# A decoder layer's feed-forward blocks of seven products: one of the three weight sums is made by an accumulating DMA, the other three partial sums are split in one instruction

## What is computed

```python
def swiglu(x, w_gate, w_up, w_down):
    return (jax.nn.silu(x @ w_gate) * (x @ w_up)) @ w_down
...
h = layer_norm(ALPHA * h + 0.5 * swiglu(h, ffn1_w_gate, ffn1_w_up, ffn1_w_down), ln1_g, ln1_b)
mix = hybrid_mixer(h, ...)          # SSD branch, sliding-window attention, gated merge, output projection
h = layer_norm(ALPHA * h + mix, ln2_g, ln2_b)
h = layer_norm(ALPHA * h + 0.5 * swiglu(h, ffn2_w_gate, ffn2_w_up, ffn2_w_down), ln3_g, ln3_b)
```

## Time and profile before

| | us |
|---|---|
| median of 3 runs | 2670.63 |
| lowest, highest | 2668.64, 2671.52 |
| the profiled execution | 2668.99 |
| its span, first to last instruction | 2667.4 |
| PE busy in it | 2634.5 (99%) |
| DVE busy | 2002.6 (75%) |
| ACT busy | 1361.7 (51%) |
| mean granted TensorE clock | 0.996 |

### The profile page before, as it was taken

One profiled execution on the slowest core, in us unless ns is written; L12 is line 12 of the kernel. 1 busy time (PEld: TensorE's weight loads), 2 busy tenths in 40 slices (PEclk: granted clock), 3 DMA queues, 4 the chain that ended last, 5 costly groups with the idle time before them and its releaser, 6 DMA issues.

```text
span 2667.4 us, 36687 instructions
## 1 busy us (share of the span) xinstructions
PE 2634.5 (99%) x12546; PEld 2188.8 (82%) x12546; DVE 2002.6 (75%) x2410; ACT 1361.7 (51%) x1678; POOL 130.0 (5%) x170
## 2 busy tenths in 40 slices
PE   8999999999999999999999999999999999999997
PEld 7888888888787788888888888888878888888886
DVE  6999997688666665677777765444689999977986
ACT  5555555455344454566555554444355555554553
POOL 1000000000000000211111100000000000000000
PEclk9999999999999999999999999999999999999999
DMA  6666566666655546665555565667666665666664
GB/s 224 204 191 209 185 205 204 214 200 204 189 171 147 156 150 197 206 181 179 177 177 177 179 183 165 190 190 247 200 190 204 190 211 186 205 202 229 210 208 171
DMA packets 286195, 513.96 MB, mean 193 GB/s; under 512 B 19648, under 2 KB 52592, under 8 KB 284048
## 3 DMA queue, kind: packets, MB, share of 16 engines
q1 hardware_dynamic: 279552, 485.03, 57.8%
q0 software_dynamic: 4880, 25.36, 2.6%
q10 hardware_dynamic: 1664, 2.26, 0.2%
HBM read 506.23 MB, written 6.36 MB: 192 GB/s over the span
## 4 chain that ended last, share of the span: by engine, by line
PE 95%; DVE 3%; ACT 1%; issue 0%; DMA 0%; POOL 0%; POOLq 0%; SPq 0%; ACTq 0%; DVEq 0%
PE acc L787 13%; PE acc L789 13%; PE acc L788 13%; PE acc L853 5%; PE acc L855 5%; PE acc L854 5%; PE acc L871 4%; PE acc L872 4%; PE acc L873 4%; PE spare L871 4%; PE spare L872 4%; PE spare L873 4%; PE spare L855 3%; PE spare L854 3%; PE spare L853 3%; PE spare L756 2%
## 5 line engine op out<-in xcount | busy, mean ns | idle before, releaser
L1728 DVE TENSOR_TENSOR w_lo<-land,w_hi 128x1024 fp32r<-128x1024 f32 (+1 forms) x956 | 1149.2, 1219 | 499.4 <-ACT w_hi L1309 490.6
L1309 ACT ACTIVATE w_hi<-land 128x1024 fp32r<-128x1024 f32 (+1 forms) x956 | 976.8, 1029 | 916.9 <-PE acc L789 328.0
L787 PE MATMUL acc<-w_hi,a_hi 128*128 128x512 f32 (+1 forms) x1184 | 451.2, 381 | 2.6 <-DVE a_lo L1775 1.8
L789 PE MATMUL acc<-w_hi,a_lo 128*128 128x512 f32 (+1 forms) x1184 | 435.8, 368 | 0.0
L788 PE MATMUL acc<-w_lo,a_hi 128*128 128x512 f32 (+1 forms) x1184 | 434.4, 367 | 0.0
L787 PEld LDWEIGHTS acc<-w_hi,a_hi 128*128 128x128 f32 x1184 | 223.9, 189 | 46.8 <-issue 9.2
L789 PEld LDWEIGHTS acc<-w_hi,a_lo 128*128 128x128 f32 x1184 | 223.6, 189 | 38.2
L788 PEld LDWEIGHTS acc<-w_lo,a_hi 128*128 128x128 f32 x1184 | 224.1, 189 | 37.4 <-issue 3.6
L853 PE MATMUL acc<-w_hi,a_hi 128*128 128x512 f32 x576 | 227.7, 395 | 2.0 <-DVE a_lo L1775 1.7
L855 PE MATMUL acc<-w_hi,a_lo 128*128 128x512 f32 x576 | 225.1, 391 | 0.0
L854 PE MATMUL acc<-w_lo,a_hi 128*128 128x512 f32 x576 | 225.0, 391 | 0.0
(11 more groups left out here) (388 smaller groups left out, 4233.1 us busy)
## 6 DMA issues: line engine op xcount, KB each, us to landing
land<-w_in SPq DMA_DIRECT2D x232, 512.0 KB, 3.9
land<-ffn_w_gate SPq DMA_DIRECT2D x176, 512.0 KB, 3.9
land<-ffn_w_up SPq DMA_DIRECT2D x176, 512.0 KB, 4.3
land<-ffn_w_down SPq DMA_DIRECT2D x176, 512.0 KB, 4.7
land<-w_ssd_o SPq DMA_DIRECT2D x64, 512.0 KB, 4.3
land<-w_in SPq DMA_DIRECT2D x132, 128.0 KB, 2.3
land<-w_attn_o SPq DMA_DIRECT2D x32, 512.0 KB, 4.1
land<-w_out SPq DMA_DIRECT2D x32, 512.0 KB, 4.4
```

What stands on the lines that cost most here:

```text
L787: pe.matmul(to, rows_hi, hi, start=first, stop=False)
L789: mm = pe.matmul(to, rows_lo, hi, start=False, stop=last)
L1309: act.activation(w_hi[:, l % SPLIT, 0:deep, 0:width], land[:, l % LAND, 0:deep, 0:width], ACT.Copy).then_inc(high, 1)
L1728: dve.tensor_tensor(w_lo[:, l % SPLIT, 0:deep, 0:width], land[:, l % LAND, 0:deep, 0:width], w_hi[:, l % SPLIT, 0:deep, 0:width].bitcast(F ...
```

## The change

U0+U1 is no longer a DVE addition. After the first sum (now G0+U0, written to `t_sums` and not in place) POOL issues a DMA that reads U1 from HBM a second time, 256 KB, and adds it onto U0 in the landing buffer (`add_third`). The ordinary split of the up slab then splits (U0+U1, U1). ACT waits for that DMA (`third_added`) before it splits the up slab. The three sums that stay on DVE are contiguous in `t_sums`, and their high parts are made by one ACT instruction of 128x1536 and the low parts by one of DVE. Both stand ahead of the up slab's split in their engine's order, and PE takes the three products of the partial sums ahead of the two of the up slab.

```diff
+            def add_third(slot, n, block):
+                pool.wait_ge(sums, n * 3 + 1)
+                pool.dma_start(land[:, slot, 0, :], block, accum_op=ALU.add).then_inc(third_added, 16)
...
+            up_thirds(1)
             refill_late(1, x_view)
             hidden_complete(1)
             pool.dma_start(resid[:, :, 0:2 * W], x_view[:, :, 0:2 * W]).then_inc(resid_in, 16)
+            down_thirds(1)
...
                 pe.wait_ge(rest, slab_at + 1)
                 three(aux[:, 0, :], rows_of(0, 0), block(lg, 0), first, last)
                 three(own[:, 0, :], rows_of(1, 0), block(lg, 1)).then_inc(used, 1)
+                pe.wait_ge(t_rest, n + 1)
+                three(aux[:, 1, :], mixed_rows(1), t_block(0), first, last)
+                if turned is not None:
+                    pe.wait_ge(gt_out, turned)
+                three(aux[:, 3, :], mixed_rows(2), t_block(1), first, last)
+                three(own[:, 1, :], rows_of(1, 1), t_block(2)).then_inc(t_used, 1)
                 pe.wait_ge(rest, slab_at + 2)
                 three(own[:, 2, :], mixed_rows(3), block(lu, 1))
-                three(aux[:, 1, :], mixed_rows(1), block(lu, 0), first, last).then_inc(used, 1)
...
+                three(aux[:, 2, :], mixed_rows(0), block(lu, 0), first, last).then_inc(used, 1)
...
-                        act.wait_ge(sums, n * 4 + 2)
-                        split(f"up{f}", i, l)
+                    if n is not None and l % 2 == 1:
+                        act.wait_ge(third_added, n * 16 + 16)
+                    split(f"up{f}", i, l)
+                    if n is not None and l % 2 == 0:
                         t_high_parts(n, "up")
...
-                dve.tensor_tensor(sz[:, 0, :], up[:, 0, :], up[:, 1, :], ALU.add).then_inc(sums, 1)
-                dve.wait_ge(sums, n * 4 + 1)
-                dve.tensor_tensor(up[:, 0, :], gate[:, 0, :], up[:, 0, :], ALU.add).then_inc(sums, 1)
-                dve.wait_ge(sums, n * 4 + 2)
-                dve.tensor_tensor(sz[:, 1, :], up[:, 0, :], up[:, 1, :], ALU.add).then_inc(sums, 1)
-                dve.wait_ge(sums, n * 4 + 3)
+                dve.tensor_tensor(sz[:, 0, :], gate[:, 0, :], up[:, 0, :], ALU.add).then_inc(sums, 1)
+                dve.wait_ge(sums, n * 3 + 1)
+                dve.tensor_tensor(sz[:, 1, :], sz[:, 0, :], up[:, 1, :], ALU.add).then_inc(sums, 1)
+                dve.wait_ge(sums, n * 3 + 2)
                 dve.tensor_tensor(t_four, sz[:, 1, :], gate[:, 1, :], ALU.add).then_inc(sums, 1)
...
-                    split(f"up{f}", i, l)
                     if l // 2 in SEVEN and l % 2 == 1:
                         t_low_parts(seven_block(f, i, l // 2), "up")
+                    split(f"up{f}", i, l)
```

More of the change, by code:

```diff
@@ L349, in build_decoder_layer @@
         state = placed("state", [P, W], F32, 94 * K)
-        sz = sb("sz", [P, TOK, W])
-        bcT = sb("bcT", [P, 2, SEQ])
+        t_sums = sb("t_sums", [P, 3, W])
+        sz = t_sums[:, 0:TOK, :]
+        t_four = t_sums[:, TOK, :]
+        bcT = t_four.rearrange("p (k n) -> p k n", k=2)
         b_tok = sb("b_tok", [P, P])
@@ L651, in refill_late, with up_thirds, chunk, down_thirds @@
                 pool.dma_start(resid[:, :, 2 * W:], view[:, :, 2 * W:]).then_inc(resid_late_in, 16)
+            def add_third(slot, n, block):
+                pool.wait_ge(sums, n * 3 + 1)
+                pool.dma_start(land[:, slot, 0, :], block, accum_op=ALU.add).then_inc(third_added, 16)
+            def up_thirds(f):
+                def chunk(i):
+                    for b in SEVEN:
+                        add_third((2 * b + 1) % LAND, seven_block(f, i, b), ffn_w[f][1][:, 2 * b + 1, bass.ds(i * W, W)])
+                for i in range(1, ALONE + 1):
+                    chunk(i)
+                with pool.Fori(1, 1 + (NC_S - ALONE) // 2) as m:
+                    for k in range(2):
+                        chunk(m * 2 + (ALONE - 1 + k))
+            def down_thirds(f):
+                for j in range(2):
+                    for l, (p, c) in enumerate(DOWN_SLABS[j]):
+                        s = DOWN_ORDER[j][p]
+                        if s in DOWN_SEVEN and c == 1:
+                            at = (2 * j + 1) * W
+                            add_third(l % LAND, down_block(f, j, DOWN_SEVEN.index(s)),
+                                      ffn_w[f][2][:, 2 * s + 1, at:at + W])
+            up_thirds(1)
             refill_late(1, x_view)
@@ L1414, in t_high_parts @@
             def t_high_parts(n, t_set):
-                hi, hi_four, _, _ = t_of[t_set]
-                act.wait_ge(sums, n * 4 + 3)
+                act.wait_ge(sums, n * 3 + 3)
                 if not is_zero(n):
                     act.wait_ge(t_used, n)
-                act.activation(hi[:, :, :], sz[:, :, :], ACT.Copy).then_inc(t_high, 1)
-                act.wait_ge(sums, n * 4 + 4)
-                act.activation(hi_four[:, :], t_four, ACT.Copy).then_inc(t_high, 1)
+                act.activation(t_of[t_set][0][:, :, :], t_sums[:, :, :], ACT.Copy).then_inc(t_high, 1)
             def copy_one(f, i, odd):
-                act.wait_ge(t_used, seven_block(f, i, SEVEN[-1]) + 1)
+                act.wait_ge(used, slab_no(f"up{f}", i, 2 * SEVEN[-1] + 1) + 1)
                 act.activation(q_one, chunk_banks(1 - odd)[:, 0, :], ACT.Copy).then_inc(q_copied, 1)
@@ L1457, in copy_one_down @@
             def copy_one_down(f, j):
-                act.wait_ge(t_used, down_block(f, j, len(DOWN_SEVEN) - 1) + 1)
+                last = 2 * DOWN_ORDER[j].index(DOWN_SEVEN[-1]) + 1
+                act.wait_ge(used, slab_no(f"down{f}", j, last) + 1)
                 if j == 1:
@@ L1475, in down @@
                             copy_one_down(f, 1)
[L1476 to L1479, removed]
+                        n = down_block(f, j, DOWN_SEVEN.index(s)) if s in DOWN_SEVEN else None
+                        if n is not None and c == 1:
+                            act.wait_ge(third_added, n * 16 + 16)
+                        split(f"down{f}", j, l)
+                        if n is not None and c == 0:
                             t_high_parts(n, "down")
-                        else:
-                            split(f"down{f}", j, l)
             ffn(1, "xT", None)
@@ L2080, in down @@
                             block_sums(phase, j, l, n)
-                        split(phase, j, l)
                         if n is not None and c == 1:
                             t_low_parts(n, "down")
+                        split(phase, j, l)
                 evacuate_down(f, 1, 0)
```

50 lines of the change are left out of this document (18 added, 32 removed).

## The result

| | before | changed |
|---|---|---|
| median, us | 2670.6 | 2740.4 |
| lowest to highest | 2668.6 to 2671.5 | 2739.7 to 2740.7 |
| ratio, 95% interval | | 1.026 (1.024 to 1.028) |

What follows compares the result with a forecast made beforehand. PE was taken to bound the kernel. DVE's saving at nothing, 13 us in the up phase and 10 in the down phase sum to 23 us, on the median 2670.6: 2694 us; range 2668 to 2785.

Steps and rivals of the forecast that it cites:

- PE bounds, DVE's saving is worth nothing: Whole kernel: PE sets the time; 63 us less DVE work gains nothing, at most PE's 2.2 us of waits.
- X = 4.6 us: Third sum's DMA, all 74 blocks: time from issue to landing, put at 4.6 us with ends 3.1 and 6.3.
- predicted loop: First sum to next block's first sum through DMA, splits and reload: 11.8 us against PE's own 10.2.
- Third block of a chunk, 13 us: Up phase: PE waits there for partial sums and up slab, 0.7 us per chunk, times 18 chunks, 13 us.
- First block of a chunk, 0 us: Up phase: hidden values' low parts arrive just in time for PE, slack having come back in ordinary slabs; no cost.
- Down phase, 10 us: Fifth block of each half: partial sums and up slab late for PE, 2.4 us per half, times 4, 10 us.
- Hidden: Rival: third sum's DMA lands in under about 4.3 us, cost under 6 us, time 2669 to 2676; chance 0.32.
- A slow accumulate: Rival: third sum's DMA takes above 5.8 us because rows don't overlap, time above 2782; chance 0.18.
- The extra traffic: Rival: third sums' 19 MB delay the weight loads, 10 us more; put into the range, no chance of its own.
- The check list: Signs expected in the profile after: POOL, ACT and PE waits by place, DVE busy about 63 us less, PE busy unchanged.

Runs made afterwards that it cites:

- the hidden values ahead: Changed kernel, but in each chunk's first block ACT and DVE split the hidden values ahead of the up slab and its DMA wait: 2737.4 us, ratio 1.0255.
- traffic only: Changed kernel, but DVE makes the third sum and the 74 accumulating DMAs go onto a tile nobody reads, only POOL waiting: 2688.5 us, 1.0071.

## Where the prediction was right and where it failed

*PE bounds, DVE's saving is worth nothing: right.* By its groups of instructions DVE lost 61.6 us (74 sums of 692 ns, and 140.6 - 130.2 on the low splits), as foreseen (63). The page's busy time fell by 46.6 only. It counts once what neighbouring instructions overlap: all DVE instructions added up fell by 58.2 (2116.6 to 2058.4), and what overlaps fell from 114.0 to 102.4. No kernel gained from less DVE work; the merged split alone is at 0.9999.

*X = 4.6 us: close.* The median is 4.2 and the mean over the 74 is 4.4. The prediction had added 3.6 for the doubled traffic and 1.0 for a neighbour; together that is 0.4 too much at the median, and no run tells which of the two. Missing was the handoff from DVE to POOL, 0.63 us in the loop over chunks, which the prediction put "in the rounding". The reload took 3.75 and not 4.1 in this stretch. That the three errors cancel is luck: predicted loop 7.2 + 4.6 = 11.8, measured 11.8 and 11.9 in the up phase (means over 18 chunks).

*Third block of a chunk, 13 us: right in place and kind, the size by luck.* PE is late there for `t_lo` and `w_lo`, at the places named: 11.1 us over the 18 chunks, with what PE loses when it starts again (last section). But the forecast let PE reach that block without a stop. In fact the first sum had lost 1.1 us of its lead over PE by the first block (below), and PE's stop there gave back 1.4. So at the third block the first sum leads by 4.0 us (mean of 16 chunks), near the 344.62 - 341.04 = 3.6 of the prediction. Counted over the chunk PE is 2.1 us late and not 0.7.

*First block of a chunk, 0 us: this step failed.* The prediction said that the slack "comes back in the ordinary slabs, where DVE waits for PE", so that A(1) is the same in every chunk, and that the hidden values are then "just in time". Measured: the loss in first blocks is 26 us, the largest part of all. In the timeline above A(1) is 330.28, and PE's block starts here:

```profile
335.64 0.39 PE L900 MATMUL acc<-w_hi,a_hi 128*128 128x512 f32 x1
...
337.45 0.39 PE L902 MATMUL acc<-t_hi,s_lo 128*128 128x512 f32 x1
339.38 0.50 PE L900 MATMUL acc<-t_hi,s_hi 128*128 128x512 f32 x1 [1.54 <-DVE g_lo L1909]
```

The first sum leads PE's block by 335.64 - 330.28 = 5.36 us. Before it led by 324.22 - 317.44 = 6.78. (Over 16 chunks the means are 5.7 and 6.8.) The hidden low parts are ready 9.05 us after the first sum (338.05 + 1.28); predicted were 8.9. So the position behind the first sum was forecast to 0.2 us, and nearly the whole of the 1.7 us by which this matmul starts late is the 1.4 us of lead that did not come back. It shows in 17 of the 18 chunks, 1.4 us each on average.

Why it doesn't come back stands in the same timeline. Before the change ACT, and DVE behind it, wait for PE in this stretch, as the prediction said:

```profile
309.93 1.06 ACT L1309 ACTIVATE w_hi<-land 128x1024 fp32r<-128x1024 f32 x1 [1.17 <-PE acc L855]
312.71 1.06 ACT L1309 ACTIVATE w_hi<-land 128x1024 fp32r<-128x1024 f32 x1 [1.72 <-PE acc L855]
```

In the changed kernel, from the late split of the third block's up slab on, they don't:

```profile
314.54 3.90 ACT L1337 ACTIVATE w_hi<-land 128x1024 fp32r<-128x1024 f32 x4 [1.93 <-DMA land<-ffn_w_up]
...
321.17 1.06 ACT L1337 ACTIVATE w_hi<-land 128x1024 fp32r<-128x1024 f32 x1 [1.97 <-DMA land<-ffn_w_up]
323.30 1.06 ACT L1337 ACTIVATE w_hi<-land 128x1024 fp32r<-128x1024 f32 x1 [1.06 <-DMA land<-ffn_w_gate]
324.90 1.06 ACT L1337 ACTIVATE w_hi<-land 128x1024 fp32r<-128x1024 f32 x1 [0.54 <-DMA land<-ffn_w_up]
```

The late up slab and the three landed slabs behind it are split in one run (DVE's "x4" at 315.63). So all four buffers come free within 4 us and are reloaded in a row, from 316.88 on:

```profile
316.88 0.37 SPq L504 DMA_DIRECT2D land<-ffn_w_up  x1
318.15 0.37 SPq L504 DMA_DIRECT2D land<-ffn_w_gate  x1
319.15 0.37 SPq L504 DMA_DIRECT2D land<-ffn_w_up  x1
320.42 0.37 SPq L504 DMA_DIRECT2D land<-ffn_w_gate  x1
```

Then there is nothing landed to split until 321.17, the slabs come about 2 us apart, and the closing of the previous chunk (325.53 in DVE's timeline, 4.75 us ahead of A(1) in both kernels) stands behind them. DVE waits for the loads there and not for PE. The lateness of the third block is thus handed to the next chunk's first. The distances of the first sums show the loop as a whole (means, us):

| | block 1 to 2 | 2 to 3 | 3 to next 1 | a chunk |
|---|---|---|---|---|
| before | 10.3 | 9.7 | 22.6 | 42.5, PE's own pace |
| DMA in blocks 1 and 2 only | 11.8 | 12.0 | 19.9 | 43.6 |
| changed | 11.8 | 11.9 | 21.1 | 44.8 |

Only 1.5 us of the 3.7 lost over two blocks are made up in the long stretch. The middle row suggests that 1.2 us of the 21.1 come with the third block's own DMA, which the prediction left out of the way to the next chunk. That the rest is held up by the reload in a burst is read from this timeline; no kernel tested it. PE has to follow a loop that is 2.2 us longer, and its late starts in up blocks are 37.0 / 18 = 2.1 us a chunk. The experiment with the hidden values ahead confirms it from the other side: the loop keeps its length (44.7), and the loss keeps nearly its size under other names.

*Down phase, 10 us: mechanism right, size a third.* Its late starts rose by 31 us (1.4 to 32.7). Some 10 of them are the order (11.9 without any DMA), which the prediction mentioned ("the change takes slack in any case") but did not price, and 5 more the traffic (17.2 with traffic only). That leaves 15 for the wait, where 10 were forecast. Five first sums of one half stand at 555.24, 568.56, 581.56, 593.30 and 606.24 in the changed kernel:

```profile
555.24 0.69 DVE L1955 TENSOR_TENSOR t_sums<-land 128x512 f32<-128x512 f32 x1 [0.16 <-DMA land<-ffn_w_down]
568.56 0.69 DVE L1955 TENSOR_TENSOR t_sums<-land 128x512 f32<-128x512 f32 x1 [1.56 <-DMA land<-ffn_w_down]
581.56 0.69 DVE L1955 TENSOR_TENSOR t_sums<-land 128x512 f32<-128x512 f32 x1 [2.52 <-DMA land<-ffn_w_down]
```

The mean distance is 12.75 us in this half and 12.0 over the four, not 11.8. A reason at hand is that the `w_down` slabs take 4.9 us to land (median; 4.1 was taken for all). PE is late in every block from the third on at the latest, not just in the fifth. In this phase a single stop of 3.3 us close to the end is included. It is there with 3.6 us in the kernel without any DMA as well:

```profile
PE acc L896 <- DVE w_lo L1748: 4.7, 2, 3.6
```

It comes some 20 us after POOL issues its loads of the rows for the last normalization (`last_rows`). The kernel before and the one with the old order on ACT and DVE issue these at the same place and have no such stop, so it takes the new order; whether the loads have a part in it was not tested.

*The rivals.* Hidden did not come, though a wait of 3.3 us would have left little more than the 18 us of order and traffic. A slow accumulate did not come. The extra traffic was put into the range with 10 us, on top of the forecast, and measured 9: it should have stood in the sum, since both its reads were taken as certain. The size agrees by luck, though: 7 of the 10 were to come in the up phase, and the kernel with traffic only has 1.7 us of late starts in up blocks.

*The check list.* "POOL's waits, ACT waiting for a DMA, PE waits longest in the third block": true but for the longest, which are in the first. "PE busy unchanged": it rose by 26.5 us, from waits that hide under drawn matmuls and from restarts. "None in the first block of a down half": true but for 0.2 us in the last half.

## What to carry to other kernels

When one instruction in a loop over few buffers gets longer, compare the length of the whole loop, over a full period of the schedule, with the bounding engine's pace; slack comes back only where the late engine waits for the bounding one, and a row that shows it doing so before the change doesn't show that it still will when it is late. A stretch that had slack before can lose it to the lateness itself, here where buffers freed in a burst are refilled in a burst. A DMA in place of a 0.7 us vector instruction costs a handoff, an issue and a transfer, 5 us here; where a buffer's reload waits for it, the loop needs that much slack.

## What the runs showed of the hardware

**An accumulating DMA costs its destination too.** For the same 74 transfers of 256 KB the software queue's line reads without them, as a copy, and as a sum (packets, MB, share of 16 engines; the spans of the last two differ by 2%):

```profile
q0 software_dynamic: 4880, 25.36, 2.6%
```

```profile
q0 software_dynamic: 10800, 44.76, 4.9%
```

```profile
q0 software_dynamic: 15536, 44.76, 7.4%
```

The copy adds 2.3% of queue time in 5920 packets, the sum 4.8% in 10656, with the same bytes counted: twice the time. It lands in 4.2 us against 3.3, 0.33 us of it a longer issue (0.865 against 0.537). The Trainium skill has this for collectives (*Collectives: The Full Stack*, "The bandwidth ceiling: the fold count and why AG ≠ RS ≠ AR": two reads per chunk, half the rate of a copy); the trace agrees with it for a plain accumulating DMA in queue time, 4.8% against 2.3%. By the fit of the Trainium skill for POOL's transfers (*DMA: Bandwidth & Descriptors*, "Anatomy of one DMA — SWDGE (gpsimd) path") 256 KB would take an estimated 2.6 us; the copy took 3.3 here beside the loads, and the measurement decides.

**From DVE to POOL it is 0.3 us, and 0.6 in a loop.** From the end of the first sum to the start of POOL's issue the median is 0.30 us at the DMAs written out one by one (chunk 1 and the down phase), and 0.63 us in POOL's loop over the chunks (341.96 + 0.69 to 343.28). In the loop POOL's sequencer runs two more instructions of line 654 between the wait and the DMA, 48 times each, presumably for the address, and the first of them starts 0.04 us after the sum's end:

```profile
L654 POOLq FUSED_REGOPS  x48: 42/43/57, 106.5 to 2410.4; - x48
```

The kernel with the sum from SBUF has the loop written out and 0.29 or 0.30 us in the same chunks. So 0.3 us of each of 48 waits come from the loop and not from the DMA. A kernel with that changed alone was not run.

**A PE that stopped loses 0.11 us more.** The first matmul after a wait is drawn 0.50 us long and the next one starts 0.34 us later and not 0.227, as at 339.38 above. The changed kernel has some 95 more of them than the kernel before, which makes about 10 us of the 68.4; no wait shows them.
